# Products without a reader added to TensorE's queue in nine places of a two-layer diffusion trunk

## What is computed

```python
h = rmsnorm(x, p["g_pre1"]) * (1.0 + sc1) + sh1
dq, dk, dv, sz, sxbc, sdt, nq, nk, nv = split_in(h @ p["w_in"])
# A differential attention, B bidirectional SSD scan, C neighbourhood attention
mix = (ga * (o_da @ p["w_br_da"]) + gs * (o_ssm @ p["w_br_ssm"]) + gn * (o_na @ p["w_br_na"])) @ p["w_out"]
x = x + g1 * rmsnorm(mix, p["g_post1"])
h2 = rmsnorm(x, p["g_pre2"]) * (1.0 + sc2) + sh2
x = x + g2 * rmsnorm(moe_ffn(h2, p), p["g_post2"])
```

## Time and profile before

| | |
|---|---|
| runs shown | 2882.38, 2883.58, 2887.42 us |
| median | 2883.58 us |
| profiled execution, its own time | 2886.92 us |
| its span | 2885.1 us |
| mean granted clock of PE | 0.929 |
| PE busy | 2504.8 us (87%) |
| DVE, ACT, POOL busy | 943.9, 598.6, 366.5 us |
| bytes moved | 357.95 MB, 124 GB/s on average |

### The profile page before, as it was taken

One profiled execution on the slowest core, in us unless ns is written; L12 is line 12 of the kernel. 1 busy time (PEld: TensorE's weight loads), 2 busy tenths in 40 slices (PEclk: granted clock), 3 DMA queues, 4 the chain that ended last, 5 costly groups with the idle time before them and its releaser, 6 DMA issues. The chain is left out here.

```text
span 2885.1 us, 36073 instructions
## 1 busy us (share of the span) xinstructions
PE 2504.8 (87%) x13898; PEld 1503.4 (52%) x13898; DVE 943.9 (33%) x1837; ACT 598.6 (21%) x1392; POOL 366.5 (13%) x390
## 2 busy tenths in 40 slices
PE   4999989879999989788739998986999998979885
PEld 2446544456457645444325555545655864645442
DVE  1414312453016334322335142136410632332225
ACT  2221101430014012122142121025001401202221
POOL 0005100021002100133100250000300120013330
PEclk8999999899989999899869999989999899889998
DMA  8441044100542030677743101110032203064785
GB/s 312 145 151 37 30 164 176 37 1 30 200 140 48 30 115 37 260 284 287 283 147 101 62 30 49 57 66 1 30 124 96 51 30 114 37 252 159 279 327 187
DMA packets 170108, 357.95 MB, mean 124 GB/s; under 512 B 35076, under 2 KB 56684, under 8 KB 169972
## 3 DMA queue, kind: packets, MB, share of 16 engines
q1 hardware_dynamic: 129812, 267.70, 26.2%
q10 hardware_dynamic: 22176, 46.37, 4.6%
q0 software_dynamic: 17984, 42.01, 4.0%
HBM read 331.60 MB, written 47.48 MB: 131 GB/s over the span
## 5 line engine op out<-in xcount | busy, mean ns | idle before, releaser
L226 PE MATMUL ps<-hT,ring 128*128 128x512 f32 x896 | 411.2, 613 | 13.1 <-PEq L2822 11.9
L226 PEld LDWEIGHTS ps<-hT,ring 128*128 128x128 f32 x896 | 172.2, 197 | 228.9 <-issue 228.7
L2300 PE MATMUL ps<-ring,mixT 128*32 128x256 f32 x2688 | 223.3, 388 | 7.0 <-issue 7.0
L235 PE MATMUL ps<-ring,hT 128*128 128x512 f32 x480 | 212.2, 600 | 8.4 <-PEq L1182 7.4
L2300 PEld LDWEIGHTS ps<-ring,mixT 128*32 128x32 f32 x2688 | 126.2, 113 | 109.0 <-issue 48.5
L1220 POOL TENSOR_TENSOR mix_S<-ring 128x512 f32<-128x512 f32 x16 | 25.3, 1579 | 1169.6 <-POOLq L1357 606.1
L2184 PE MATMUL ps<-ring,mixT 128*128 128x512 f32 x320 | 142.9, 607 | 20.5 <-PEq L2822 20.5
L235 PEld LDWEIGHTS ps<-ring,hT 128*128 128x128 f32 x480 | 91.3, 192 | 122.4 <-issue 120.3
L1269 PE MATMUL ps<-late,ring 128*128 128x320 f32 x512 | 145.1, 442 | 5.6 <-PEq L1698 2.5
L2318 PE MATMUL ps<-ring,ex_hidT 128*32 128x512 f32 x768 | 123.1, 628 | 23.4 <-issue 11.6
L1269 PEld LDWEIGHTS ps<-late,ring 128*128 128x128 f32 x512 | 98.4, 193 | 50.3 <-issue 11.6
(11 more groups left out here) (436 smaller groups left out, 3895.9 us busy)
## 6 DMA issues: line engine op xcount, KB each, us to landing
ring<-in_w_in SPq DMA_DIRECT2D x18, 2048.0 KB, 9.1
ring<-in_w_gate SPq DMA_DIRECT2D x12, 2048.0 KB, 9.7
ring<-in_w_e_down SPq DMA_DIRECT2D x48, 512.0 KB, 13.9
ring<-in_w_e_gate SPq DMA_DIRECT2D x40, 512.0 KB, 7.2
ring<-in_w_e_up SPq DMA_DIRECT2D x40, 512.0 KB, 8.0
co_yg<-y_rows SPq DMA_DIRECT2D x40, 512.0 KB, 6.8
mixT<-in_w_ada ACTq DMA_DIRECT2D x8, 2048.0 KB, 8.9
da_ada_w<-in_w_ada ACTq DMA_DIRECT2D x8, 2048.0 KB, 8.8
```

The costliest lines, as they stand in the source:

```text
L226: pe.matmul(lat, wide[:, k, c], hT[:, k, CTX:TOK], start=(k == 0), stop=(k == kt_n - 1))
L235: last = pe.matmul(out, cx.hT[:, k, tok(t)], wide[:, k, :], start=(k == 0), stop=(k == KT - 1))
L2300: ins = pe.matmul(ps[rows, 2 + b, 0:2 * P].rearrange("p (g f) -> p g f", g=2), xT[:, b, k, rows], ew[:, :, k, :], start=(k == 0), stop=(k ...
```

## The change

A helper issues n products of the identity by the first four tables of `base` (128 x 512) into one PSUM bank, with no semaphore; nothing reads them. It is called in nine places of PE's queue: 34 products ahead of everything else in `stage_first`; 10 ahead of the wait for `y_normed`; 9 at the end of `stage_mix_s`; 3 (branch a) and 9 (branch n) at the end of `stage_mix`; 15 ahead of the wait for `da_normed`; 9 ahead of the wait for `na_kc_out`; 9 ahead of `place_ready`; 14 after the expert loop; and 11 after each of the five norm turns of the combination. All but the first and the last are in both layers. Waits are put before some of them so that the bank is free; in `stage_na` one wait is moved up for that.

```diff
--- before.py
+++ after.py
@@ -238,6 +238,12 @@
 
 
 
+def idle_products(cx, pe, bank, n):
+
+    for _i in range(n):
+        pe.matmul(cx.ps[:, bank, :], cx.ident, cx.base[:, 0:SEC], start=True, stop=True)
+
+
 class AdaJob:
 
 
@@ -460,6 +466,7 @@
 
         @block.tensor
         def _(pe):
+            idle_products(cx, pe, 7, 34)
             pe.wait_ge(sem("c_silu"), 1)
             for i in range(4):
                 wide = section_ready(cx, pe, ("ada", i))
@@ -815,6 +822,8 @@
             gate_lat(7)
             gate_ctx(7)
 
+            pe.wait_ge(sem("seg_exp"), 2 * TILES)
+            idle_products(cx, pe, 2, 10)
             pe.wait_ge(sem("y_normed"), 1)
             for m in range(4):
                 if m >= 2:
@@ -1153,6 +1162,8 @@
                     sem("mix_s_mm"), 1)
             pe.wait_ge(sem("mix_s_mm"), KT)
             pe.sem_inc(cx.ring_free, 1)
+            pe.wait_ge(sem("mix_s_out"), KT - 3)
+            idle_products(cx, pe, 0, 9)
 
         @block.vector
         def _(dve):
@@ -1279,6 +1290,8 @@
             pe.wait_ge(name("branch_mm"), PAIRS)
             for _i in range(2):
                 pe.sem_inc(cx.ring_free, 1)
+            pe.wait_ge(name("c12"), PAIRS)
+            idle_products(cx, pe, 0, 3 if n == 0 else 9)
 
         @block.scalar
         def _(act):
@@ -1513,6 +1526,7 @@
                 turn(u)
             values(len(units) - 1)
 
+            idle_products(cx, pe, 6, 15)
             pe.wait_ge(sem("da_normed"), 1)
             for h in range(DA_H):
                 if h >= 2:
@@ -1799,9 +1813,10 @@
             for c in range(4):
                 ins = pe.transpose(ps[:, 1, c * P:(c + 1) * P], kT[:, c, 0:CTX], cx.ident)
             ins.then_inc(sem("na_kc_turned"), 1)
+            pe.wait_ge(sem("na_v_out"), TILES)
+            idle_products(cx, pe, 6, 9)
             pe.wait_ge(sem("na_kc_out"), 1)
             pe.wait_ge(sem("na_k_staged"), 1)
-            pe.wait_ge(sem("na_v_out"), TILES)
             pe.wait_ge(sem("na_cache_v"), 16)
 
             def scores(g):
@@ -2266,6 +2281,7 @@
             ins.then_inc(sem("ids_turned"), 1)
             pe.wait_ge(sem("rows_high_out"), TILES)
             shared(1, 0)
+            idle_products(cx, pe, 3, 9)
             pe.wait_ge(sem("place_ready"), 1)
             for n in range(N_CHOICE):
                 ins = pe.matmul(ps[:, 3, 0:TABLE], place[:, n, :], where[:, n, :], start=(n == 0),
@@ -2336,6 +2352,8 @@
                             pe.wait_ge(sem(f"down_full{s % 2}"), LANES * 16 * (s // 2 + 1))
                         down(n, i, s)
                 first = last
+            pe.wait_ge(sem("xT_low"), last * UNROLL + 1)
+            idle_products(cx, pe, 0, 14)
 
         @block.scalar
         def _(act):
@@ -2657,6 +2675,8 @@
             if more:
                 for t in range(TILES):
                     turn_norm(t)
+                    pe.wait_ge(sem("co_first"), 3)
+                    idle_products(cx, pe, 4, 11)
 
         @block.scalar
         def _(act):
@@ -2789,6 +2809,7 @@
         def sb(name, shape):
             return st.enter_context(nc.sbuf_tensor(name, shape, F32))
         base = sb("base", [P, 7 * P])
+        cx.base = base
         cx.fold = sb("fold", [P, 32])
         cx.eps = sb("eps", [P, 1])
         cx.eps4 = sb("eps4", [P, 1])
```

## The result

Measured in turn with the kernel before, the changed kernel takes 2936.09 us (median of four, 2923.35 to 2944.25) against 2882.98 (2880.61 to 2887.42): ratio 1.018, 95% interval 1.0157 to 1.0203, so +45 to +59 us. The forecast was 2928, with a range of its own of 2912 to 2943, and slower. The profiled execution took 2923.35 us, with a span of 2921.6: it is the fastest of the four, and its mean granted clock of 0.968 the highest (the others: 0.957 to 0.961). So its trace lies only 36.5 us above that of before, where the medians lie 53 apart.

What follows compares the result with a forecast made beforehand. PE, busy 87% of the span, was taken to bound the kernel. Overruns and barrier costs less clock gains summed to +44.3 us, a median of 2928 us; own range 2912 to 2943, with the rivals near no change 2882 to 2946.

Steps and rivals of the forecast that it cites:

- The barrier: At block ends the barrier waits for PE's queued products: mix_s +6.8, branch n +4.3, expert loop +1.7 us per layer.
- no row of PE decides: The prediction's remark that no profile row shows whether a barrier waits for PE's queued products; it argued from DVE's row.
- Both rivals in which the barrier passes: Barrier passes over PE's queue: 2886 us, chance 0.11; the same with neighbourhood units' clock staying up: 2873 us, chance 0.05.
- The price of a product: One filler call is two records of 0.43 us: 0.86 us at full clock, twice that at half.
- The rival of 0.61 us: A product costs its mean length, so fillers end about when the waits do: 2882 us, chance 0.07.
- y_normed, da_normed, branch a, place_ready: Fillers at these four sites: y_normed +1.2, da_normed +1.9, place_ready -2.6 us per layer; branch a -2.9, first layer alone.
- The rival in which identity products or transposes don't hold the clock: Clock falls again in transposes, 2939 us, or identity products don't hold it at all, 2951 us; chance 0.07.
- The neighbourhood scores: Nine products ahead of na_kc_out end 3.2 and 6.9 us late; 0.9 won by the clock, sum +9.2 us.
- The norm turns: First layer's combination: turns take 10.3 us with eleven products, and the fifth filler lies ahead of a barrier: net +11.4 us.
- The start: 34 products at the kernel's start: groups end 0.9 us later, small products gain 3.9; bounds -3.6 and +4, taken as 0.
- The sum: All sites together +44.3 us, taking the median to 2928 us; forecast's chance 0.70.
- The sign named for PE's busy time: PE's busy time was to rise by some 210 us, from 245 calls of 0.86 us.

Runs made afterwards that it cites:

- The doubled filler: Changed kernel with only the filler at the end of mix_s, 18 products instead of 9, every other count 0: 2909.99 us, ratio 1.0095.
- the timed kernel: Changed kernel with one filler kept: under scores, only the scores' 9 products, 2895.68 us, ratio 1.0048; under start, only the 34 products, 2885.0 us, ratio 1.0016.
- the second profile of the changed kernel: The changed kernel run once more with no edit: 2927.27 us, ratio 1.0175.
- the fifth filler alone: Read in the run of the changed kernel with only block-end fillers (mix_s, branch n, expert loop, fifth norm turn): 2914.48 us, ratio 1.012.
- 58 well-placed products: Changed kernel with only y_normed 6, da_normed 10, three in each branch, place_ready 7, every other count 0: 2866.11 us, ratio 0.9941.
- the sized kernel: Changed kernel with every filler cut to what its wait holds at 0.86 us a product: 2862.12 us, ratio 0.9934.

## Why the prediction was right, and where it was off

**The barrier (+6.8, +4.3, +1.7 a layer, and the fifth turn).** Right, and the largest part of the result. The one row of evidence, DVE's last merge in the earlier trace rows, was read rightly. But "no row of PE decides" was wrong: the DRAIN rows of the kernel before decide it, 1395 ns long while the transposes are in work and 13 ns when PE is idle. The doubled filler shows it again: a microsecond of products ahead of the barrier is a microsecond later. The sizes were low by 0.2 to 0.7 us: nine products last 7.96 us to the end of the last record, not 7.7, and begin a little after the last projection (384.42 against 384.27). Both rivals in which the barrier passes are out.

**The price of a product (0.86 us).** Right: 18 records take 7.96 us and 36 take 15.69, 0.43 us more for each. The rival of 0.61 us is out, though 601 ns is what the page gives as the mean of one.

**y_normed, da_normed, branch a, place_ready.** By the table all within some 0.5 us of the forecast, the sum for y_normed 0.6 above it. For branch a I took -2.9 in the first layer alone, since only there rows showed the loss. That was the luck of one trace too: in the seven traces without this filler the work behind it starts at half clock in 9 of 14 cases (four times in layer 0, five in layer 1) and costs some 3 us more, in the six with it in none of 12. So it is worth some 2 us in each layer. The rival in which identity products or transposes don't hold the clock is out: behind the filler the first ten transposes start 0.13 us apart.

```profile
336.89 8.82 PE L244 MATMUL ps<-base 128*128 128x512 f32 x20
345.55 1.25 PE L834 MATMUL ps<-base,ssm_xs 128*128 128x128 f32 x10
```

By the Trainium skill (TensorE: Matmul & The Clock Gate, Part 4: PE-mode transpose) transposes don't lift the clock; here they neither kept it from rising nor let it fall behind a filler (20 of them from 345.55 to 348.39, all at 1.00).

**The neighbourhood scores (+9.2).** The step that failed is "I take 0.9, near the low end", and behind it the reading of one trace: that the clock "stays down for 24 us" was taken for a property of the kernel. It varies from one execution to the next, with and without the filler. By the traces the term is some +3.6 (0.1 and 3.5 by the means), by the timed kernel +14 (8 to 19). The two don't quite agree; with four executions timed and five and four profiled, the true size stays open between 4 and 14, and 9.2 lies in it. The comparison of the two traces, -8.2, is the one reading that is refuted.

**The norm turns (+11.4).** Right: 11.4 in the second profile of the changed kernel, 12.6 in the first, where the first turn lasts 11.5 us and only the other three the 10.3 of the forecast. The 7.2 of the fifth filler alone, instead of 6.5, are no fault of the step: part of it ran at half clock there (22 records in 10.14 us).

**The start (0).** Too low: by 1.3 us in the two traces, 3.1 by the means of eleven, 5 (0 to 10) by the timed kernel. The first half of the step held, the four groups end late (46.93 instead of 45.46). The gain set against it, "7.74 us at half clock and 3.8 at full", didn't come:

```profile
47.10 7.74 PE L484 MATMUL ps<-fold,first_t 128*128 128x2 f32 x32 [0.17 <-PE ps L475]
```

Two windows over them in the changed kernel, then one of the kernel before:

```profile
47.10:49.60 2.50, 2.50 (x11) 2.50 (x11) 0.00 (x0) 0.49 (x1) 0.00 (x0) 0.99 1.05 386
49.60:54.80 5.20, 5.20 (x23) 5.16 (x22) 0.00 (x0) 0.00 (x0) 0.00 (x0) 0.50 1.04 387
```

```profile
46.70:47.70 1.00, 1.00 (x6) 1.00 (x5) 0.00 (x0) 0.00 (x0) 0.00 (x0) 0.50 1.03 381
```

It failed twice over. The clock that the filler had brought to 1.00 fell again at 49.6 us, in the midst of these products, though PE reads as busy throughout. And while it was up the pace was the same: 11 records in 2.5 us against 23 in 5.2. PEld is busy all the time at either level, and the whole takes 7.74 us in both kernels.

**The sum.** +44.3 against +53 (45 to 59). Start (+1.3 to +5), turns (0 to +1.2), block ends (+2.4) and y_normed (+0.6) make up 4 to 9 of the 9 us, and the scores, 5 below to 5 above their 9.2, can add to that or take from it. An interval of 14 us tells no more; that the sum came so close is in part luck. The sign named for PE's busy time, +210 us, was wrong by its own logic: it counted the fillers and forgot that whatever else they lift to full clock gets shorter.

## What to carry to other kernels

A filler pays for what the clock wins behind it and costs each microsecond by which it outlasts its wait: count its spacing, not its mean record, and end it before the wait does (the two shown last ended 0.2 and 0.3 us early). Here 58 well-placed products win 17 us where 245 lose 53. Put none ahead of a barrier beyond what another engine's tail covers, since the barrier waits for work that nobody reads. Before reading a gain off two traces, look whether the stretch has the same clock in a third and a fourth.

## What was not expected of the hardware

The spread between executions goes with TensorE's clock, and its size depends on the kernel: time and mean granted clock correlate with -0.99 over ten executions without block ends' fillers, -0.95 over ten of the sized kernel, -0.75 over 27 of the kernel before. Over 27 executions the kernel before lay between 2871.03 and 2893.52 us at clocks of 0.929 to 0.937; the sized kernel, over ten, between 2846.88 and 2877.75 at 0.952 to 0.966. The Trainium skill (TensorE: Matmul & The Clock Gate, Part 1) calls the moment at which the clock rises run-variable, and reckons what the slow start costs at under 1% of a typical kernel's span. Here the distance from the fastest to the slowest execution is 0.8% in the kernel before and 1.1% in the sized one, and one stretch of 63 to 74 us alone moves by up to 11 us.

The 32 small products follow each other at 0.24 us at 1.2 and at 2.4 GHz alike, with their weight loads, whose columns lie eight elements apart in SBUF, back to back. At 2.4 GHz, products of 128x16 whose weights lie side by side take 0.12 us each. Busy DMA engines aren't the reason: at a DMA share of 1.05 and full clock, loads of side-by-side weights take 190 ns in the changed kernel (line 235, 735 to 742 us) and these 335. That the stride is the reason is an inference; no run here changes it.
